# Last pairs of the expert layers: unsplit fp32 on the way back, and the layer norm behind them in other steps

## The reference

```python
def _expert_choice_ffn(u, w_router, w_g, w_u, w_d):
    b, n, _ = u.shape
    cap = CAPACITY_FACTOR * n // N_EXPERTS          # 64
    logits = jnp.einsum('bnd,de->ben', u, w_router, preferred_element_type=jnp.float32)
    aff = jax.nn.softmax(logits, axis=1)
    gate, idx = lax.top_k(aff, cap)
    bidx = jnp.arange(b)[:, None, None]
    xe = u[bidx, idx]
    hg = jnp.einsum('becd,edf->becf', xe, w_g)
    hu = jnp.einsum('becd,edf->becf', xe, w_u)
    ye = jnp.einsum('becf,efd->becd', jax.nn.silu(hg) * hu, w_d) * gate[..., None].astype(u.dtype)
    return jnp.zeros_like(u).at[bidx, idx].add(ye)
...
        f_lat = _expert_choice_ffn(_modulate(h_lat, m_lat[3], m_lat[4]), w_router[layer],
                                   w_exp_gate[layer], w_exp_up[layer], w_exp_down[layer])
        h_lat = _post_norm(h_lat, m_lat[5] * f_lat, ln_ffn_g[layer], ln_ffn_b[layer])
```

## Time and profile before

| | us |
|---|---|
| median of 3 runs | 2931.26 (2930.99 to 2935.04) |
| span of the profiled execution | 2932.9 |
| TensorE busy | 2717.6 (93%) |
| VectorE busy | 1156.8 (39%) |
| ScalarE busy | 813.5 (28%) |
| GpSimd busy | 119.7 (4%) |

### The profile page before, as it was taken

How to read it: one execution, slowest core, us unless ns; L and a number is a source line. 1 busy time by engine, 2 the same in 40 slices (tenths; PEclk the granted TensorE clock), 3 DMA queues, 4 the chain that set the end, 5 groups by cost and what they waited for, 6 DMA issues and landing times.

```text
span 2932.9 us, 32767 instructions
## 1 busy us (share of the span) xinstructions
PE 2717.6 (93%) x13760; PEld 1779.9 (61%) x13760; DVE 1156.8 (39%) x1700; ACT 813.5 (28%) x1249; POOL 119.7 (4%) x120
## 2 busy tenths in 40 slices
PE   6898899998899989998879999999999999999998
PEld 4555444433378544343337777878778766787886
DVE  4465512211264442111135654323244577532333
ACT  3253211100132121100024324212232467532222
POOL 1211100000000200000010010000010000000000
PEclk8999999999999989999999999999999899999999
DMA  8980799999922189999982203231341200132220
GB/s 305 325 282 16 284 415 428 427 422 421 419 99 108 44 342 424 423 419 428 428 329 92 86 29 115 72 124 57 107 130 41 69 1 1 65 115 86 95 85 36
DMA packets 125586, 601.03 MB, mean 205 GB/s; under 512 B 7408, under 2 KB 12848, under 8 KB 100608
## 3 DMA queue, kind: packets, MB, share of 16 engines
q1 hardware_dynamic: 120128, 584.27, 50.3%
q0 software_dynamic: 5312, 14.68, 1.6%
HBM read 596.83 MB, written 2.10 MB: 204 GB/s over the span
## 4 chain that ended last, share of the span: by engine, by line
PE 75%; DMA 12%; DVE 8%; ACT 3%; issue 1%; POOL 0%; DVEq 0%; ACTq 0%; POOLq 0%
PE psum L302 72%; DMA weight_ring<-in_w_exp_down 4%; DMA scratch<-in_w_exp_down 4%; PE psum L317 4%; ACT scratch L290 3%; DVE scratch L252 3%; DMA scratch<-in_w_exp_up 2%; DMA weight_ring<-in_w_exp_up 2%; DMA weight_ring<-in_w_mod 1%; DVE scratch L265 1%; DVE scratch L3773 1%; DVE h L252 1%; DVE scratch L1448 0%; DVE scratch L1947 0%; DVE scratch L1945 0%
## 5 line engine op out<-in xcount | busy, mean ns | idle before, releaser
L302 PE MATMUL psum<-scratch,scratch 128*128 128x512 f32 (+12 forms) x9404 | 1869.6, 397 | 64.7 <-DVE scratch L252 18.4
L302 PEld LDWEIGHTS psum<-scratch,scratch 128*128 128x128 f32 (+5 forms) x9404 | 1365.2, 178 | 539.3 <-issue 203.6
L302 PE MATMUL psum<-weight_ring,scratch 128*64 128x512 f32 (+2 forms) x2752 | 649.7, 612 | 71.8 <-DMA weight_ring<-in_w_exp_down 29.8
L290 ACT ACTIVATE scratch<-psum 128x512 f32<-128x512 f32 (+5 forms) x384 | 221.6, 577 | 1037.7 <-PE psum L317 554.8
L302 PEld LDWEIGHTS psum<-weight_ring,scratch 128*64 128x64 f32 (+2 forms) x2752 | 210.0, 141 | 457.7 <-issue 372.5
L252 DVE TENSOR_TENSOR scratch<-weight_ring,scratch 128x2048 fp32r<-128x2048 f32 (+2 forms) x110 | 241.9, 2199 | 480.2 <-ACT scratch L290 478.6
L290 ACT ACTIVATE scratch<-weight_ring 128x2048 fp32r<-128x2048 f32 (+2 forms) x122 | 218.7, 1793 | 570.3 <-PE psum L302 547.2
L252 DVE TENSOR_TENSOR scratch<-scratch,psum 128x512 f32<-128x512 f32 x92 | 63.3, 688 | 511.8 <-PE psum L302 510.4
L252 DVE TENSOR_TENSOR scratch<-scratch,scratch 128x512 fp32r<-128x512 f32 (+13 forms) x359 | 198.3, 552 | 63.1 <-ACT scratch L290 43.2
L317 PE MATMUL psum<-consts,scratch 128*128 128x128 f32 x1116 | 168.5, 291 | 37.1 <-DVE scratch L252 20.2
L252 DVE TENSOR_TENSOR scratch<-psum,scratch 64x512 f32<-64x512 f32 (+7 forms) x109 | 77.6, 712 | 306.8 <-PE psum L302 302.3
(11 more groups left out here) (107 smaller groups left out, 721.7 us busy)
## 6 DMA issues: line engine op xcount, KB each, us to landing
weight_ring<-in_w_exp_down SPq DMA_DIRECT2D x46, 2048.0 KB, 13.8
weight_ring<-in_w_exp_up SPq DMA_DIRECT2D x43, 2048.0 KB, 15.7
weight_ring<-in_w_exp_gate SPq DMA_DIRECT2D x42, 2048.0 KB, 15.7
weight_ring<-in_ffn_w SPq DMA_DIRECT2D x28, 2048.0 KB, 7.7
weight_ring<-in_w_mod SPq DMA_DIRECT2D x24, 2048.0 KB, 9.6
scratch<-in_w_exp_gate SPq DMA_DIRECT2D x22, 2048.0 KB, 15.8
scratch<-in_w_exp_up SPq DMA_DIRECT2D x21, 2048.0 KB, 15.8
scratch<-in_w_exp_down SPq DMA_DIRECT2D x18, 2048.0 KB, 14.2
```

The source lines that it names most:

```text
L290: A.eng.activation(out, in_, fn, **kw).then_inc(*A.mark(*names))
L302: ins = T.eng.matmul(out, lhsT, rhs, start=start, stop=stop)
```

## The change

1. `gates_pe` fetches the gates of the last pair (7) once for each expert and each half of the partitions, with 64 columns of the slot table, so that both halves hold the gates of either expert: 16 matmuls in place of 4. Pairs 4 to 6 stay.
2. `down_dve` multiplies experts 14 and 15 by row and gate in one step from PSUM, and their numbers are no longer split: ScalarE and VectorE have nothing more to do for `high` and `low` there.
3. The last part of the way back is pair 7 alone, one fp32 matmul a job. Pair 6 goes with the part before for jobs 4 to 7 (which now waits for expert 13's split), and for jobs 0 to 3 in a new step "near" into the "out" bank behind the addition of `h`.
4. Two additions and two near jobs stand ahead of expert 14's down projection, two additions ahead of expert 15's and two near jobs behind it (`AHEAD = 4`). Jobs 4 to 7 take banks of their own (7, 3, 2 and 6 behind the first), outside of the turn.
5. The norm: the root takes epsilon as its bias, and the mean is negated in a step beside it; the shift is then a product of two numbers. `POOLED` falls back to 2, so VectorE adds the bias for tiles 2 and 3.
6. Layer 1: ScalarE takes squares, roots and makes the diagonals; VectorE only the reciprocals; the first unit's low part goes to GpSimd, behind its bias additions. The order of ScalarE's steps is new: the unit's high part after tile 0's norm, the wait for TensorE's end after tile 1's.

```diff
@@ SumNorm
-    POOLED = NT - 1
-
+    def stats(self, V, t):
+        b = t % 2
+        for half in range(2):
+            x = self.combine(V, t, half)
+            V.wait_ge(*V.last())
+            V.eng.bn_stats(self.st[:, b, half, :], x).then_inc(*V.mark())
+        V.wait_ge(*V.last())
+        V.eng.bn_aggr(self.mv[:, b, :], self.st[:, b, :, :]).then_inc(*V.mark((self.key, "var", t)))
+        tt(V, self.mv[:, b, 0:1], self.mv[:, b, 0:1], self.minus, ALU.mult)
+
+    def root_act(self, A, t):
+        b = t % 2
+        A.wait_ge(*self.k.at(self.key, "constants"))
+        A.wait_ge(*self.k.at(self.key, "var", t))
+        act(A, self.r[:, b, :], self.mv[:, b, 1:2], ACT.Sqrt, (self.key, "root", t), bias=self.eps, scale=1.0)
+
+    def finish(self, V, t):
+        b = t % 2
+        V.wait_ge(*self.k.at(self.key, "root", t))
+        recip(V, self.r[:, b, :], self.r[:, b, :])
+        tt(V, self.mv[:, b, 1:2], self.mv[:, b, 0:1], self.r[:, b, :], ALU.mult, (self.key, "shift", t))
@@ SumNorm.norms_dve
             self.stats(V, t)
+            if after and 0 < t < NT - 1:
+                self.gained(V, t - 1)
             self.finish(V, t)
-            if not after:
-                continue
-            if t == NT - 1:
-                after.mean(V, 0, 1)
-            if t:
-                self.gained(V, t - 1)
+            if after and t == NT - 2:
+                after.inverse(V, 0)
         if after:
-            after.diagonals(V, 0, 1)
-            self.gained(V, NT - 1)
+            self.gained(V, NT - 2)
+            self.gained(V, NT - 1, lambda: after.inverse(V, 1))
@@ Experts
-    PARTS = ((0, 4), (4, 6), (6, 8))
-    AHEAD = 6
+    PARTS = ((0, 4), (4, 6))
+    AHEAD = 4
@@ Experts.order
+            if e == E - 1:
+                yield from (("plus", j) for j in jobs[:2])
+                yield from (("near", j) for j in jobs[:2])
             if e:
                 yield "down", e - 1
...
-        yield from (("plus", j) for j in jobs[:2])
+        yield from (("plus", j) for j in jobs[2:self.AHEAD])
         yield "down", E - 1
-        yield from (("plus", j) for j in jobs[2:self.AHEAD])
+        yield from (("near", j) for j in jobs[2:self.AHEAD])
         yield from (("back", (2, *j)) for j in jobs)
@@ Experts.act
-        self.down_act(A, E - 1)
         after = self.after
         for t in range(NT):
-            if after and t == NT - 1:
-
+            self.norm.norm_act(A, t)
+            if after and t == 0:
+                after.units.hi(A, 0)
+            if after and t == 1:
                 A.wait_ge(*k.at("end", self.end_key, "pe"))
                 after.square(A, 0)
-            self.norm.norm_act(A, t)
+                after.quick_root(A, 0, self.eps)
+            if after and t == NT - 2:
+                after.diagonal(A, 0)
@@ Experts.dve
-            after.units.lo(V, 0)
+            after.inverse(V, 2)
+            after.inverse(V, 3)
             after.chunks_dve(V)
@@ Experts.pool
             for t in range(NT):
                 self.norm.norm_pool(G, t)
+            self.after.units.lo(G, 0)
@@ Experts.gates_pe
+        if pair == E // 2 - 1:
+            for e in range(2):
+                for half in range(2):
+                    for t in range(NT):
+                        end = t == NT - 1
+                        mm(T, bank[64 * half:64 * half + 64, 2 * e:2 * e + 2],
+                           self.onehot[g][:, t, pr * P + 64 * e:pr * P + 64 * e + 64].bitcast(F32), self.aff[:, t, 2 * pair:2 * pair + 2],
+                           t == 0, end, *([("full", key, "gates", *job)] if end and e and half else []))
+            return
@@ Experts.down_dve
+            if e >= E - 2:
+                stt(V, out, bank, self.slot_gate[rows_, e:e + 1], row, ALU.mult, ALU.mult, *names)
+            else:
+                tt(V, out, bank, row, ALU.mult, *names)
+        if e >= E - 2:
+            return
@@ Experts.back_pe
+        if i == len(self.PARTS):
+            name = (self.end_key, "out", t, half)
+            if 2 * t + half >= self.AHEAD:
+                self.plus_pe(T, (t, half))
+            T.wait_ge(*k.at(self.key, "y", E - 1, half))
+            mm(T, k.psum.of(name), self.slotsT[:, E // 2 - 1, t * P:(t + 1) * P].bitcast(F32), self.y[:, half * HALF:(half + 1) * HALF],
+               False, True, ("full", *name))
+            return
         p0, p1 = self.PARTS[i]
+        if i and 2 * t + half >= self.AHEAD:
+            p1 += 1
+        T.wait_ge(*k.at(self.key, "y split", 2 * p1 - 1))
@@ Experts.plus_pe
+        i = 2 * t + half
+        if i == 0:
+            self.first_bank = k.psum.turn[0, 8]
+        own = {4: 7, 5: 3, 6: 2, 7: 6}.get(i)
+        if own is None:
+            bank = k.psum.take(T, (self.end_key, "out", t, half))
+        else:
+            b = (self.first_bank + own) % 8
+            bank = k.psum.take(T, (self.end_key, "out", t, half), (b, b + 1))
```

More of the change, by code:

```diff
@@ L2251, in back_pe @@
             end = pair == p1 - 1
[L2252 to L2253 removed]
+            mm(T, bank, s, self.high[:, pair, 4 * half:4 * half + 4, :], pair == p0 and first, False)
+            mm(T, bank, s, self.low_of(pair)[:, half * HALF:(half + 1) * HALF], False, end and bool(names), *(names if end else ()))
     def plus_pe(self, T, job):
```

78 lines of the change are left out of this document (41 added, 37 removed).

## The result

| | us |
|---|---|
| kernel after, median of 6 runs | 2942.51 (2938.11 to 2948.07) |
| kernel before in the same comparison, median of 6 | 2935.08 (2930.99 to 2938.39) |
| ratio after / before | 1.0029, 95% interval 1.0019 to 1.0039 |
| span of the profiled execution | 2936.3 |

A forecast was written before the change was run, and what follows sets the result against it. Transfers and TensorE alternate as the bound in the experts; behind T a chain of engines without transfers. 2.4 + 2.8 - 0.8 + 0.5 = +4.9 on the median 2931.26 gave 2936 us; 2930 to 2940 held 8 in 10.

The forecast's parts named there:

- Part 1: Gates of the last pair, expert 8: 16 half-width matmuls replace 4, 1.2 us a layer, +2.4 us in all.
- the half-width row: Profile row used to price the gates: half-width weight loads, four together, pass in 0.05 us each, two a matmul.
- Part 2: Tail, experts 13 to 15: waiting for expert 13's split makes TensorE late, moving T 1.4 us a layer, +2.8 us.
- T: Moment when TensorE ends expert 15's last down piece, 1514.72 and 803.41; the chain behind it has no transfer.
- rival (a): Half clock in the tail after the standstill ahead of expert 15: 1.7 us per layer affected, 2938 to 2939.5; chance 0.2.
- the row ahead of 778.74: Profile row held against rival (a): TensorE stood 2.23 us ahead of 778.74 and it cost nothing.
- The sign that it named: Sign for rival (a): the piece behind the middle part takes over 4 us.
- Part 3: Layer 0 behind T: last tile's transposes begin at T + 16.2 instead of T + 16.9; -0.8 us (0 to -1.6).
- Part 4: Layer 1 behind T: VectorE steps wait for GpSimd, next stage at T + 32.8 instead of T + 32.2; +0.5 us.
- (b): No collision of VectorE and GpSimd for single numbers: layer 1's term behind T becomes -3.5, 2932; chance 0.12.
- (d): Change does what it shortens: (b) and (c) together, 2929; with T unmoved and layer 0's full -1.6, 2926; chance 0.06.
- (c): TensorE's lateness stays hidden: gates at 0.5 and T at +0.5 a layer, 2933; chance 0.12.

The follow-up runs named there:

- the gates alone: Kernel before with only the last pair's gates made as 16 matmuls of 64 weight columns instead of 4 of 128; ratio 0.9999.
- the filled kernel: Changed kernel with 13 more matmuls a layer, results overwritten, ahead of the wait for expert 13's split; median 2938.71, ratio 1.0013.
- The way back alone: Changed kernel with norms, diagonals and weight split as before, so the kernel before with the new way back and new gates; ratio 1.0011.
- the norms alone: Kernel before with only the new norms: roots take epsilon, diagonals on ScalarE, weight split on GpSimd; ratio 1.0010.
- three edits: Changed kernel with middle part's second half between expert 15's gate and up pieces, one-number products on ScalarE, weight split on VectorE; ratio 0.9990, again 0.9988.
- the middle part moved: Changed kernel with the middle part for rows 256 to 511 put between expert 15's gate and up pieces; median 2938.10, ratio 1.0012.

## Why the prediction was wrong

**The level it was put on.** The forecast added +4.9 to 2931.26, the median of three runs. Later medians of the same kernel are 2935.08 (6 runs), 2934.45 (32), 2935.74 (27), 2935.62 (35) and 2935.19 (27): the level was 3 to 4 us too low, as the three times that were shown, 2930.99 to 2935.04, would have allowed. That is over half of the 6.5 us by which 2942.51 lies above the forecast. Put on 2935.1, the same sum is 2940.0. What is left, 2.5 us, is 1.4 by which the sum was too small and 1.1 by which this median lies above the sum as it is worked out at the end of this section. The sum is that close only because parts 1 and 2 are wrong in opposite directions (1.7 too much, 2.4 too little), which is luck.

**Part 1, gates: +2.4 forecast, +0.7 found.** The step that failed is the choice of 1.2 us a layer. The prediction calls it near the half-width row, but that row (two loads of 0.05 us a matmul) gives 16 x 0.10 - 1.1 = 0.5, and 1.2 lies above even the 1.1 of full-width loads; its upper end, 16 x 0.27, isn't half of the matmuls at double price either, but all 16 at the price of full-width ones, partly at the lower clock. The row was nearly right: the 16 matmuls add 3.93 - 12 x 0.22 = 1.3 us in the changed kernel, 0.08 each, and the four full-width ones that they replace took 0.22 each at full clock, not 0.27. The estimate by the Trainium skill ("TensorE: Matmul & The Clock Gate", Part 2: a weight load scales with its column count) said 0.8 a layer; the measurement, 0.37, is below it too, and decides. The clock falls at that place in some executions of every kernel, old gates or new (0.81 within the group of the kernel before, 0.85 in layer 1 with the gates alone).

**Part 2, the way to T: +2.8 forecast, +5.2 found** (3.2 in layer 0 and 2.1 in layer 1, means of three traces; 2.6 in layer 1 against the two traces of the kernel before alone). The mechanism was right: a standstill of 3.5 us (3.33), no wait for the last piece, lateness passed on to T. The step that failed is "16 matmuls take 3.94, so 24 take 5.9", at full clock. They take 7.4 to 8.4. Taken into the working, TensorE's lateness of 1.2 to 1.5 us becomes 2.7 to 3.0. This is rival (a), down to its size (1.7 us a layer) and cause; it had 0.2, and its 2938 to 2939.5 stood on the same low level. It was held off with the row ahead of 778.74, where 2.23 us of idle time cost nothing, and the other row, where the same 2.23 us did, was given too little weight. The sign that it named, over 4 us for the piece behind the middle part, was the wrong one: the lower clock ended within the middle part itself, and the piece took 3.65.

**Part 3, layer 0 behind T: -0.8 forecast, -0.9 found** (21.5 against 22.4). Statistics start at T + 2.0 and the transposes are interrupted once, as forecast, but the number came in part by luck. The bank is free at T + 14.0: the last tile's norm starts at T + 13.2, and its first half already frees it. Of the 32 transposes 26 stand behind that, not 12, and they take 4.71 us, with a granted clock of 0.56 from 820 to 822, so that they end at T + 18.7, as in the kernel before. In the trace of the filled kernel the same 26 run at full clock:

```profile
820.66 3.06 PE L317 MATMUL psum<-consts,scratch 128*128 128x128 f32 x26 [1.91 <-ACT scratch L290]
```

The 0.9 us come from the first chunk: VectorE starts on it at T + 16.0, in the kernel before at T + 17.3. The way back alone gives nothing here (22.4), the norms alone 0.4.

**Part 4, layer 1 behind T: +0.5 forecast, +1.2 found**, T + 33.1 where T + 32.8 was laid out; the rest is that the kernel before has 31.9 on average, not the 32.2 of its one trace. The collisions, their number, places and the releasing steps came out as worked, and so did the bound without them: -3.5 forecast, and 28.5 against 31.9 with three edits, though there ScalarE has the small products and VectorE the weight split, so that it isn't the same kernel without its collisions. It is the place where the Trainium skill's rule ("SBUF — State Buffer", Who interferes with whom: a VectorE instruction with two SBUF inputs and a GpSimd instruction that reads SBUF shut each other out) bore fruit; the traces agree, for 128 x 1 numbers too: every product of them that was held ends within 0.02 us of GpSimd's step. Rivals (b) and (d) fall with it, and (c) with part 2.

Worked with these terms, the sum is 0.74 + 5.20 - 0.89 + 1.22 = +6.3, against 6.5 measured over three comparisons. On 2935.1 that is 2941.4.

## What to carry over

A wait put ahead of dense matmuls costs its own length and then the clock behind it; price the first group behind it at both levels of the clock, and look for a place a piece or two later where what is waited for has long been done. Beside a GpSimd step that reads SBUF, every VectorE instruction with two SBUF inputs waited for what was left of that step in these traces, however few its numbers: handing work to GpSimd moves the wait to whichever such instruction comes next, so lay out all of them before judging the move, and take single numbers to ScalarE. And put a sum of a few us on a level known to better than the sum: three runs that lie 4 us apart don't give one.

## What was new of the hardware

A product of 128 x 1 numbers, 0.16 us by itself, took 4.36 us beside a GpSimd step of 4.49. It also goes the other way: in the first attention of the kernel before, GpSimd's step of 128 x 543 numbers takes 1.09 us, and the next one, of 128 x 541, which starts while a VectorE product of 128 x 1536 runs (142.63 to 144.59), takes 2.48:

```profile
143.05 2.48 POOL L252 TENSOR_TENSOR scratch<-scratch 128x541 f32<-128x541 f32 x1
```

Reciprocals (one input in SBUF) and statistics (input in PSUM) were not held: 0.16 us, and 1.50 for two, within the same GpSimd steps. An fp32 matmul with 64 weight columns and two moving columns passed in 0.08 us, with 128 weight columns in 0.22. And 3.3 us of standstill made 24 matmuls of 5.79 us take 7.4 to 8.6 in all 14 layers traced with it, and 5.79 in both layers where 13 matmuls, their results dropped, stood in its place. Without any standstill, with the middle part moved, they took 5.79 to 5.82 in 10 layers.
